# GLA level products in 64x64 tiles, one bank per head, two bank pairs in turn; memory unit's query in another row

## The reference

```python
def layer(x, ...):
    h = rmsnorm(x, g_pre)
    (c_x, c_b, c_c, c_z, g_q, g_k, g_v, g_lr, g_z,
     s_q, s_k, s_v, s_z, m_q, m_z) = split_cols(h @ w_in)      # 3344 columns
    # A: short gated convolution, 256 channels
    # B: gated linear attention (GLA), 4 heads of 64
    log_a = log_sigmoid(g_lr @ gla_wg + gla_bg) / 16
    o_b, new_gla = gla_recurrence(g_q, g_k, g_v, log_a, gla_s)
    # C: sliding window attention, 4 query and 2 key heads of 64, window 128, rotary, sinks
    # D: attention to 256 memory tokens, 4 heads of 64
    mix = concat([a_out, b_out, c_out, d_out]) @ w_out
    return x + rmsnorm(mix, g_post), ...

def gla_recurrence(q, k, v, log_a, s0):    # per head: S_t = diag(a_t) S_(t-1) + k_t^T v_t, o_t = q_t S_t
    b = cumsum(log_a)                      # within a chunk
    attn[i, j] = sum_d q[i, d] * k[j, d] * exp(b[i, d] - b[j, d])    # j <= i
    o = attn @ v + (q * exp(b)) @ S
```

## Time and profile before

| | us |
|---|---|
| median of 3 runs | 2256.68 (2256.25 to 2257.54) |
| the profiled execution | 2257.99 |
| its span, first to last instruction | 2256.2 |
| PE busy (matmuls) | 2217.0 (98%) |
| DVE busy | 1309.3 (58%) |
| ACT busy | 896.1 (40%) |
| projections L1767, three parts | 482.1 + 484.5 + 461.6 |
| output projection L2813, w_hi and scr_r parts | 195.1 + 136.1 |

### The profile page before, as it was taken

One profiled execution on the slowest core, in us unless ns is written; L12 is line 12 of the kernel. 1 busy time (PEld: TensorE's weight loads), 2 busy tenths in 40 slices (PEclk: granted clock), 3 DMA queues, 4 the chain that ended last, 5 costly groups with the idle time before them and its releaser, 6 DMA issues. The chain is left out here.

```text
span 2256.2 us, 39965 instructions
## 1 busy us (share of the span) xinstructions
PE 2217.0 (98%) x14924; PEld 1805.2 (80%) x14924; DVE 1309.3 (58%) x2870; ACT 896.1 (40%) x2015; POOL 104.9 (5%) x179
## 2 busy tenths in 40 slices
PE   8999999999999999999999999999999999999998
PEld 4778877778788888878877878777878988887887
DVE  4467755565376755646535776556645676654542
ACT  4444233344354333434425442244435442343421
POOL 1000000000000000000000000000100000000000
PEclk9999999999999999999999999999999999999999
DMA  7111212244211122324331121232441113141322
GB/s 245 38 57 29 58 37 66 66 141 145 85 39 30 43 64 74 71 77 141 132 91 41 29 52 43 52 99 82 142 132 45 39 30 77 35 106 40 100 103 75
DMA packets 230554, 172.12 MB, mean 76 GB/s; under 512 B 56886, under 2 KB 206908, under 8 KB 230332
## 3 DMA queue, kind: packets, MB, share of 16 engines
q1 hardware_dynamic: 226100, 154.78, 24.4%
q10 hardware_dynamic: 4264, 14.78, 1.9%
HBM read 136.60 MB, written 21.93 MB: 70 GB/s over the span
## 5 line engine op out<-in xcount | busy, mean ns | idle before, releaser
L1767 PE MATMUL bank<-h_hi,w_hi 128*128 128x512 f32 (+3 forms) x2160 | 482.1, 361 | 14.8 <-issue 5.2
L1767 PE MATMUL bank<-h_lo,w_hi 128*128 128x512 f32 (+3 forms) x2160 | 484.5, 361 | 2.0
L1767 PE MATMUL bank<-h_hi,w_lo 128*128 128x512 f32 (+2 forms) x2080 | 461.6, 360 | 2.0
L1767 PEld LDWEIGHTS bank<-h_hi,w_hi 128*128 128x128 f32 (+1 forms) x2160 | 353.0, 185 | 90.0 <-issue 31.5
L1767 PEld LDWEIGHTS bank<-h_lo,w_hi 128*128 128x128 f32 (+1 forms) x2160 | 353.4, 185 | 73.1 <-issue 13.6
L1767 PEld LDWEIGHTS bank<-h_hi,w_lo 128*128 128x128 f32 x2080 | 344.2, 188 | 65.8 <-issue 14.1
L2813 PE MATMUL bank<-scr_r,tb_r 128*128 128x512 f32 x816 | 195.1, 396 | 1.0 <-issue 1.0
L2813 PEld LDWEIGHTS bank<-scr_r,tb_r 128*128 128x128 f32 x816 | 151.7, 188 | 35.7 <-issue 2.3
L2138 ACT ACTIVATE tb<-bank 128x512 f32<-128x512 f32 (+1 forms) x140 | 71.3, 509 | 218.0 <-PE bank L1767 207.8
L2294 ACT ACTIVATE scr<-bank 128x1024 f32<-128x1024 f32 x64 | 65.7, 1027 | 194.7 <-PE bank L2045 194.7
L2875 ACT ACTIVATE junk<-bank 128x512 bf16<-128x512 f32 x68 | 40.6, 597 | 240.9 <-PE bank L2813 231.2
(11 more groups left out here) (297 smaller groups left out, 2911.6 us busy)
## 6 DMA issues: line engine op xcount, KB each, us to landing
w_raw<-in_w_in SPq DMA_DIRECT2D x96, 512.0 KB, 3.8
out<-scr SPq DMA_DIRECT2D x32, 512.0 KB, 2.7
scr<-in_w_out SPq DMA_DIRECT2D x16, 512.0 KB, 5.2
w_raw<-in_w_out SPq DMA_DIRECT2D x16, 512.0 KB, 3.8
scr<-in_x_prompt SPq DMA_DIRECT2D x16, 512.0 KB, 3.6
scr<-out SPq DMA_DIRECT2D x16, 512.0 KB, 3.3
rot<-out ACTq DMA_DIRECT2D x12, 512.0 KB, 3.6
mix_t<-in_x_prompt ACTq DMA_DIRECT2D x8, 512.0 KB, 13.8
```

The costliest lines, as they stand in the source:

```text
L1767: m = mm(bank[b][0:m_w, 0:c1 - c0], w[:, slot, k, 0:m_w], h[:, k, c0:c1], start=it["piece"] == 0 and k == 0, stop=it["piece"] == 2 and k = ...
```

## The change

`gla_g` and `gla_f` become one item `gla_p` (p). One head's plain product and all its levels stand in one bank (128 columns for the plain product, with level 64 in its upper right quarter, 64 for level 32, 5 x 64 for the fine levels: 512). Chunks use banks 2 and 3, and 4 and 5, in turn. The tokens of a chunk are split in halves of 64: each product is made for a token half by itself, as a 64x64 tile of the array (head by row half, token half by column half), with 32 columns streamed at a level and 64 for the plain product. Only level 64 joins the two halves: its weights are the first half's keys, 64 columns streamed. So a chunk has 4 + 2 + 24 matmuls in place of 2 + 4 + 10. ACT copies level 32 only (2 copies a chunk); level 64 is copied with the diagonal, whose mask has level 64 added. o waits for the copies as before. The planner emits, for chunk c, o(c), then t(c+2) where c is even, then p(c+2), and forecasts 1.1 us for a p on PE. D's query moves from row 0 to row 1, and the row rules are derived from `SLOT`. The low parts of the weights stay on VectorE.

```diff
-        ("D", "q"): 0, ("D", "z"): 3}
+        ("D", "q"): 1, ("D", "z"): 3}
...
-            p = run("PE", 0.33 if small else 0.88, self.needs(it))
-            q = p if small else run("ACT", 0.7, p)
-            at[("coarse", n, c)] = q = run("DVE", 0.55 if small else 0.72, q)
-            self.free(q, 4, 5)
-        elif k == "gla_f":
-            p = run("PE", 0.49 if small else 1.22, self.needs(it))
-            at[("attn", n, c)] = q = run("DVE", 1.1 if small else 2.15, p)
-            self.free(q, 2, 3)
+            p = run("PE", 0.82 if small else 1.1, self.needs(it))
+            q = p if small else run("ACT", 0.5, p, when(("o", n, c - 2)))
+            at[("attn", n, c)] = q = run("DVE", 1.6 if small else 2.8, q)
+            self.free(q, *it["bank_list"])
...
-            for c in range(chunks + 1):
+            for c in range(-2, chunks):
+                if c >= 0:
+                    last = item("gla_o", banks_o, step=s, c=c)
...
+                    out.append(last)
+                if c + 2 < chunks:
                     if c % 2 == 0:
-                        out.append(item("gla_t", [6], step=s, c=c))
+                        out.append(item("gla_t", [6], step=s, c=c + 2))
+                    out.append(item("gla_p", [4, 5] if c % 2 else [2, 3], step=s, c=c + 2))
...
-            link(nc.vector.tensor_copy(diag_mask[:], level_f32[:, NL, :]))
+            link(nc.vector.tensor_tensor(diag_mask[:], level_f32[:, NL, :], level_f32[:, 0, :], ALU.add))
...
+                    for tk in halves:
+                        for h, hp in enumerate(heads):
+                            mm(dst[h][tk, tk], k[hp, tk], q[hp, tk], start=True, stop=True)
+                    if HD in levels:
+                        x = e_row(s, 1 + levels.index(HD))[:, tok]
+                        for h, hp in enumerate(heads):
+                            mm(dst[h][0:HD, HD:w], x[hp, 0:HD], x[hp, HD:w], start=True, stop=True)
                     for n, v in enumerate(levels):
-                        if v < COARSE:
+                        if v == HD:
                             continue
                         x = e_row(s, 1 + n)[:, tok]
-                        for h, hp in enumerate(heads):
-                            last[h] = mm(compact(coarse_of(h, n), v), x[hp], pairs(x[hp], v)[:, :, 1, :],
-                                         start=True, stop=True)
...
+                        for i, tk in enumerate(halves):
+                            o = at + HD // 2 * i
+                            for h, hp in enumerate(heads):
+                                m = mm(compact(dst[h][tk, o:o + HD // 2], v), k[hp, tk] if v == 1 else x[hp, tk],
+                                       pairs(x[hp, tk], v)[:, :, 1, :], start=True, stop=True)
+                                if v == 1 and tk is halves[-1]:
+                                    m.then_inc(bank_full[it["bank_list"][h]], 1)
...
                     pe.wait_ge(attn_done, it["seq"] + 1)
-                    pe.wait_ge(coarse_done, it["seq"] + 1)
...
+                        for t0 in range(0, CH, 2 * COARSE):
+                            o = CH + t0 // 2
+                            fn(a[t0:t0 + COARSE, :, t0 + COARSE:t0 + 2 * COARSE], psum[t0:t0 + COARSE, b0:b0 + 2, o:o + COARSE], ACT.Copy)
```

More of the change, by code:

```diff
@@ L192, in needs @@
                  "fac_prod": [("exp", n, it.get("i", 0)), ("q", n), ("k", n)],
[L193 to L194 removed]
+                 "gla_p": [("factors", n)],
                  "gla_t": [("kd", n), ("v", n)],
@@ L393 @@
 PART_US = {"soft": 3.5, "scale": 1.4, "fac_exp": 1.1, "spread": 0.5, "held": 2.2}
-ROWS = {"A": (1, 2, 3), "B": (0, 1, 2, 3), "C": (0, 1, 2, 3), "D": (0, 3)}
+ROWS = {u: {r for (v, _), r in SLOT.items() if v == u} for u in "ABCD"}
+ROWS["C"].add(2)
 def last_reader(s, row, with_sample):
@@ L406, in last_reader @@
     end = 0 if u["st"] == "s" else ST // CH - 1 if u["unit"] == "B" else PAIRS - 1
[L407 to L408 removed]
     if u["unit"] == "A":
[L410 to L417 removed]
+        if row == SLOT[("A", "x")]:
+            if with_sample and u["st"] != 0:
+                return ("conv_out", u["n"], 0), u
+            return ("evict", u["n"], "x"), u
+        return ("evict", u["n"], "z"), u
+    if row == SLOT[(u["unit"], "z")]:
+        return (("gla_norm", u["n"], 0) if u["unit"] == "B" else ("value", u["n"], end)), u
+    if u["unit"] == "D":
+        return ("score", u["n"], end), u
+    kind, c = {"B": (("gla_p", end), ("gla_p", end), ("gla_t", end - 1)),
+               "C": (("score", end), ("rope_k", 0), ("rope_q", 0))}[u["unit"]][row]
     return (kind, u["n"], c), u
@@ L600, in emit @@
         if kind == "gla_o":
-            it["columns_first"] = it["step"]["st"] != "s" and last_on_pe[0] in ("gla_f", "score", "value")
+            it["columns_first"] = it["step"]["st"] != "s" and last_on_pe[0] in ("gla_p", "score", "value")
         if kind in ON_PE:
@@ L799, in rested @@
         def rested(it, after=None):
-            if it["kind"] == "gla_g" or (p and not with_sample and after and (it["kind"], after["kind"]) in ONE_VISIT and it["step"]["st"] != "s"):
+            if (p and not with_sample and after and (it["kind"], after["kind"]) in ONE_VISIT and it["step"]["st"] != "s"):
                 return max(ready(it), ready(after)) + safe
@@ L810, in plan_units @@
         for rank, q in ((1, main if m else []), (2, side)):
-            if q and not any(bank_held(x) for x in q[:2 if q[0]["kind"] == "gla_g" else 1]):
+            if q and not any(bank_held(x) for x in q[:1]):
                 choice.append((rested(*q[:2]), rank, q))
@@ L1507, in compact, with fine_at @@
             return ap.rearrange("p (m r) -> p m r", r=v)
-        def coarse_of(h, n):
-            return bank[4 + h][:, CH + CH // 2 * n:CH + CH // 2 * (n + 1)]
+        def fine_at(s, j):
+            half = chunk(s) // 2
+            return slice(CH + CH // 2 + half * j, CH + CH // 2 + half * (j + 1))
         def groups_of(s):
@@ L1833, in on_tensor @@
                     heads = [slice(HD * h, HD * h + HD) for h in range(2)]
+                    halves = [slice(HD * j, HD * j + HD) for j in range(w // HD)]
+                    dst = [bank[b] for b in it["bank_list"]]
                     pe.wait_ge(factors_done, gate_steps.index(s["n"]) + 1)
-                    for h in range(2):
-                        emptied(pe, it, 4 + h)
-                    last = [None, None]
-                    for h, hp in enumerate(heads):
-                        last[h] = mm(bank[4 + h][0:w, 0:w], k[hp], q[hp], start=True, stop=True)
+                    for b in it["bank_list"]:
+                        emptied(pe, it, b)
@@ new lines, in on_tensor @@
+                        at = CH if v == COARSE else fine_at(s, [m for m, _ in fine_of(s)].index(n)).start
+                        for i, tk in enumerate(halves):
[5 more added lines that the diff above has]
+                                    m.then_inc(bank_full[it["bank_list"][h]], 1)
@@ L2502, in on_vector @@
                     m.then_inc(attn_done, 1)
-                    for b in (2, 3):
+                    for b in it["bank_list"]:
                         dve.drain().then_inc(bank_free[b], 1)
```

87 lines of the change are left out of this document (17 added, 70 removed).

## The result

| | before | after |
|---|---|---|
| median, measured together | 2256.61 us (6 runs) | 2274.19 us (6 runs, 2267.06 to 2279.15) |
| ratio | | 1.0072 [1.006, 1.0085] |
| profiled execution, its span | 2257.99, 2256.2 | 2267.06, 2265.3 |
| idle time of PE, summed over its gaps | 31.9 | 70.5 |
| waits of PE over 1.2 us | 5 | 22 |

A forecast was written before the change was run, and what follows sets the result against it. PE's own program order was taken as the bound. Products -55 us, shapes and visits -1, new waits +3 gave -53 us: from 2256.7 to 2204, stated as 2205, range 2194 to 2244.

The forecast's parts named there:

- What bounds the kernel: Whole kernel: PE never waits for long, so its program order is the time; longest sum of waits 5.2 us.
- Pace of the products, visits: GLA products on PE: a step of four tiles costs 0.058 us; by chunks 54 us gained, by visits 55.
- a gain of 1: Tile shape changes and fewer PE visits to GLA work: nearly cancel, leaving 1 us of gain.
- Rivals (1): GLA level products: second column half brings nothing, tiles run two at a time; 2257 us, no change; 8%.
- rival (2): PE records can't start closer than a floor, 28 ns: 2253 us (5%), or 2229 for the half (7%).
- rival (3): GLA tiles: a load can't run while the other column half of the same rows streams; 2303 us, slower; 3%.
- Rows: D's query in row 1: shifts which tiles wait for D's scores; neither end worth more than 1 us.
- New waits: PE waits brought by its shorter stream: between 0 and 10 us in all, taken as 3.
- The cover: PE before a unit's first o: 16 projection matmuls, 3.9 us, hide the wait for copied matrices.
- the share of VectorE, 87%: VectorE in the fullest stretch: busy 34.5 of 39.6 us after the change, still not the bound.
- Rival (4): GLA units: VectorE late with matrices or factors, 1.2 us per unit before o, some 20 us; 2225 us; 10%.
- The slower side: Whole kernel: chance of 0.04 that it becomes slower, above 2261 us.

The follow-up runs named there:

- e2: after's steps, banks and order, but all 128 tokens of a chunk loaded as weights (wide products): 2320.6 us.
- g1: f1's order, item for item, with e2's wide products: 2261.1 us.
- f1: after with other planner numbers only (product step 1.4 us, SAFE 0.3, RETURN_US 0.1, REST_US 2.5), so another order: 2209.6 us.
- e1: after with D's query back in tile row 0, nothing else: 2296.0 us.
- e4: after with VectorE making only an eighth of each projection weight's low part: 2265.1 us.
- g2: f1's order, item for item, with e4's edit (an eighth of each low weight part on VectorE): 2205.2 us.
- f3: before with 64x64 product tiles and the planner's two product prices lowered to 0.5 and 0.6 us: 2320.3 us; with the tiles alone 2222.0.
- f2: after with one planner number changed, the product step priced at 2.1 us instead of 1.1: 2249.1 us.

## Why the prediction failed, step by step

**What bounds the kernel.** Right for before: PE's own order is the time. But "an edit is worth what it takes out of PE's own stream" holds only as long as PE has something to put into the time that comes free. With some 50 us less in the stream, PE was left without permitted work at ten places in each layer. The reading "the longest sum is 5.2 us" also leaves out a wait of 6.8 us for the first transfer, which no order here changes.

**Pace of the products, visits.** Right. A step of four 64x64 tiles costs 0.060 us, forecast 0.058; visits 2.51, 2.35 and 1.75 against 2.54, 2.32 and 1.79. In sum the time fell by 46 us (e2 against after) or 51.5 (g1 against f1), and the work by 49.6 (ledger, before against after), where 56 were forecast. Freed of idle time and slow clock as in the ledger, g1 has 55.6 us more work than f1: what the products were to bring. But g1 has 5 us more work than before, though its products are as slow; the merged step and its visits cost that much, where the prediction had a gain of 1. Where it goes is open. Rivals (1), (2) and (3) are thereby out: 60 ns per four records is one every 15 ns, half of rival (2)'s 28 ns. The Trainium skill's floor of 25 ns between starts (TensorE: Matmul & The Clock Gate, "Wait — 56ns, not 53.3ns?") and its rule that a load overlaps a running matmul only where the row group differs (same page, "The mechanism") would have made 0.100 and 0.17 of the 0.060; the measurement decides against both, as the prediction read them, for column tiles side by side.

**Rows.** "Neither end is worth more than 1 us": the row change was worth 22 us in the new order (e1). The bound was taken from PE's waits in before's order, and a row rule doesn't act through those but through what the planner writes when the rule changes.

**New waits: the step that failed.** "Between 0 and 10 us in all; I take 3, since it is still not the bound." Measured: 38.6 us of idle time. Two things were wrong in it. The cover (16 projection matmuls, 3.9 us, ahead of an o) was read off the first unit of a pass and taken for all sixteen. In after's trace twelve units have 16 to 24, two have 12 (ahead of their second p), and the fourth of the first pass in each layer has 4; these last two units wait 7.6 us between them, before an o or for a bank whose target row is still read. Most of the other 31 us is outside the GLA units, where the prediction did not look at the order. And the share of VectorE, 87%, was used as the measure of lateness. e4 and g2 show that 84 us of VectorE's load are worth 9 and 4 us: what stood in the way was the length of chains (o, state, o; norm, end of slot, rotary, score) with nothing beside them. A forecast of them was to be had: with the planner's own numbers after has 36.2 us of gaps on PE in two layers, before 6.8. The prediction compared the order in one unit instead.

**The clock.** It had no term at all. The waits brought 54 us more at 0.5, by estimate 20 us of time.

**Rival (4)** had the sign of the waits, at 20 us and by VectorE's load; the size was 59 with the clock and the cause was the order. Its own sign, more than 10 us of waits at o, did not come (L1901 has 4.4). What did come is the last sentence's "projections start to wait for their banks", but not "because VectorE is late".

**The slower side** was given 4%, by rival (3) and "a little for anything unseen". No rival said that a shorter step makes the planner write another order, and f3 shows that this by itself can cost 98 us.

**Still open**: why f2's order is better than its forecast; and what decides whether the clock falls after a wait. It did not after 2.0 us at 1042 us in before nor after 2.9 us at 1009 us in f1, and it did after 1.57 us at 259 in after. No run tried to set the length of a wait with all else equal.

## What to carry to other kernels

Where a planner with a price table writes the order, a change of a step's length or price is a change of the whole order: walk the new order through the forecast and compare PE's gaps, the number of long ones above all, before trusting the sum of the steps, and price the order and the step in separate runs (old order with new step, new order with old step). A wait of PE that ends with VectorE says which chain is long, not that VectorE is full; relieve the engine in one run before calling it the bound. When a gain of tens of us goes missing, sum PE's gaps and the time at the low clock, since neither shows in the page's tenths.

## What was not expected of the hardware

- Four 64x64 tiles of an fp32 matmul, two row halves by two column halves, each with a new weight load, run in 60 ns a step, a record every 15 ns, sustained over 48 records.
- Waits of 1.2 to 4 us are often followed by a granted clock of 0.5 for 3.4 to 17.1 us; each us of it costs some 0.37 us in this kernel (0.34 to 0.46 by pair of kernels).
- A VectorE TENSOR_TENSOR of 0.42 us takes 2.62 us beside a POOL subtraction of 2.43 us; copies out of PSUM keep theirs in the same kernel (L2465, 354 ns in the mean, 353 in f1).
